# Head of a one-layer trunk kernel: the tiles of x loaded ahead of w_ada, and the sums over w_ada shared out anew between TensorE and VectorE

## The chip, the cores and the metric

One core of one Trainium2 chip runs the kernel. The metric is the device time in microseconds (us). TensorE (PE) multiplies matrices, PEld is its weight load, VectorE is DVE, ScalarE is ACT, GpSimd is POOL, and SP issues the loads from the chip's main memory (DRAM) into SBUF. PSUM is where TensorE writes; it has eight banks.

## The reference

`x` is 1024 x 1024 in float32, `c` one vector of 1024, `w_ada` 1024 x 6144. What follows is the start of the layer; the mixer, the output projection and the MLP come after it and are not touched by the change.

```python
c_act = jax.nn.silu(c)
mod = (c_act @ w_ada[l] + b_ada[l])[:, None, :]
sh_m, sc_m, g_m, sh_f, sc_f, g_f = jnp.split(mod, 6, axis=-1)
u = layer_norm(x) * (1 + sc_m) + sh_m
z = u @ w_in[l]
```

## The kernel before

The order of the work is written out by hand, one program for each engine; semaphores tie them together, and each engine takes its program strictly in order.

`x` comes in eight tiles of 128 rows (512 KB each, in `mid`). For each tile VectorE takes mean and variance (`stats`: two BN_STATS, one BN_AGGR, one small add), ScalarE takes the root (`take_root`), VectorE makes the reciprocal and the negative mean (`scale_bias`), ScalarE normalises the tile (`norm`, 128x1024), TensorE transposes it in eight 128x128 pieces (`transpose_x`), and ScalarE copies the transposed tile from PSUM to `x_t` (`save_tile`). VectorE normalises tile 7 itself and copies it to `x_t`.

`w_ada` comes in twelve chunks of 512 columns (2 MB each) into three buffers `ada[i % 3]`; chunk `i` has eight row blocks `k`. Chunks 0 and 1 are the shift of `u`, chunks 2 and 3 its scale; chunks 0 and 2 belong to the channel blocks k = 0 to 3 of `u`, chunks 1 and 3 to k = 4 to 7. The product with `c_act` is made in one of two ways:

- on TensorE (`row_chunk`): one matmul for each row block, `c_act` as a weight of one column, 512 columns streamed, summed into one row of PSUM; ScalarE saves that row (`save_ada_row`), and four small matmuls turn it into columns (`row_columns`);
- on VectorE (`start_chunk`, `end_chunk`): one 128x512 multiply (or multiply and add) for each row block into `partial`, and four small matmuls against ones sum over the partitions and give the same columns.

Before, chunks 0 and 2 go the first way and chunks 1 and 3 the second. From the columns VectorE makes `mod` (`mixer_columns`), ScalarE makes `u_tmp = x_t * scale + shift` and its rounded half `act_hi` (`modulate_x`), VectorE the rest `act_lo` (`cut_u_lo`). Each of the eight blocks `k` of `u` then enters the first projections: `rows_part(n, k)` is six matmuls of 512 columns (three products for each half of the rows) for weight block `n`, whose own halves come from ScalarE (`cut_hi`) and VectorE (`cut_lo`). So the projections of k = 0 to 3 wait for chunks 0 and 2, those of k = 4 to 7 for chunks 1 and 3.

Of the kernel before, what the change touches and what calls it, by code (L numbers as in the profile page):

```python
# [65 lines left out]
N_DIRECT = 2  # L66
ROW_ORDER = (0, 2, 1, 3)
ADA_BANKS = {0: 0, 2: 1}
# [7 lines left out]
def trunk_layer(nc, x, c, w_ada, b_ada, w_in, b_gate, w_pool, pool_scale, rel_bias, conv_w, conv_b,  # L76
# [173 lines left out]
    with ExitStack() as ctx:  # L250
# [229 lines left out]
        def _(sp):  # L480
# [11 lines left out]
            def load_ada(i):  # L492
                if i == 3:
                    sp.wait_ge(head_ps_done, 1)
                elif i == 4:
                    sp.wait_ge(partial_done, 1)
                elif i == 5:
                    sp.wait_ge(head_ps_done, 4)
                elif i == 6:
                    sp.wait_ge(partial_done, 2)  # L500
                elif i >= 7:
                    sp.wait_ge(partial_done, i - 2 - N_DIRECT)
                if i < 4:
                    load_ada_half(i, 0)
                    load_ada_half(i, 1)
                else:
                    sp.dma_start(ada[i % 3][:, :, :], ada_view[:, :, i * HALF:(i + 1) * HALF])\
                        .then_inc(ada_in[i % 3], 16)

            def load_ada_half(i, half):  # L510
                ks = slice(4 * half, 4 * half + 4)
# [421 lines left out]
        def _(act):  # L933
# [28 lines left out]
            def save_ada_row(i):  # L962
                act.wait_ge(head_ps_done, {0: 1, 2: 4}[i])
                copy(ada_row[i], ps[0:1, ADA_BANKS[i], :]).then_inc(head_sb_done, 1)

            def save_tile(i):
                act.wait_ge(z_done, i + 1)
                copy(x_t[:, :, i * P:(i + 1) * P], tile_banks(i)).then_inc(x_copied, 1)

            for i in range(0, ST, 2):  # L970
                take_root(i, i)
                take_root(i + 1, i + 1)
                norm(i, i, mid[:, i, :])
                if i + 1 < ST - 1:
                    norm(i + 1, i + 1, mid[:, i + 1, :])
                if i == 2:
                    save_ada_row(0)
                if i == ST - 2:
                    save_ada_row(2)
                    cut_hi(0)  # L980
                    save_tile(i)
                else:
                    save_tile(i)
                    save_tile(i + 1)
# [16 lines left out]
            cut_hi(2)  # L1001
            act.wait_ge(mod_done, 2)
# [372 lines left out]
        def _(dve):  # L1375
# [33 lines left out]
            for i in range(0, ST, 2):  # L1409
                for t in (i, i + 1):  # L1410
                    dve.wait_ge(x_in[t], 16)
                    stats(mid[:, t, :], t)
                for t in (i, i + 1):
                    scale_bias(t, t)
                if i == 4:
                    dve.wait_ge(head_ps_done, 3)
                    nc.vector.tensor_copy(cols[:, 0:ROWS_A], ps[:, 7, PIECE:PIECE + ROWS_A])
                    nc.vector.tensor_copy(cols[:, ROWS_A:ROWS_A + ROWS_C], ps[:, 7, PIECE + P:PIECE + P + ROWS_C])\
                        .then_inc(cols_done, 1)
# [8 lines left out]
            def start_chunk(i):  # L1428

                dve.wait_ge(ada_in[i % 3], 16 * (i // 3 + 1))  # L1430
# [4 lines left out]
                link(nc.vector.tensor_scalar(partial_of(i)[:, :], ada[i % 3][:, 0, :], c_act[:, 0:1], None, ALU.mult))  # L1435
                add_rows(i, range(1, 4))

            def end_chunk(i):
                if i in (1, 3):
                    dve.wait_ge(ada_end_in[i % 3], 16 * (i // 3 + 1))  # L1440
                add_rows(i, range(4, 8))
# [42 lines left out]

            mixer_columns(0)
            dve.wait_ge(z_done, ST)
            nc.vector.tensor_copy(x_t[:, :, (ST - 1) * P:ST * P], tile_banks(ST - 1)).then_inc(x_copied, 1)
# [573 lines left out]
        def _(pe):  # L2061
# [19 lines left out]
            def row_chunk(i, half):  # L2081

                pe.wait_ge((ada_in, ada_end_in)[half][i % 3], 16)
                for k in range(4 * half, 4 * half + 4):
                    ins = nc.tensor.matmul(ps[0:1, ADA_BANKS[i], :], c_act[:, k:k + 1], ada[i % 3][:, k, :],  # L2085
                                           start=k == 0, stop=k == 7)
                return ins

            def row_columns(i):

                if i in (0, 2):
                    pe.wait_ge(head_sb_done, 3 + i // 2)
                else:
                    pe.wait_ge(cols_done, 1)
                    pe.wait_ge(partial_done, 1 + i // 2)
                for m in range(4):
                    out, ms = ps[:, 6 + i % 2, 4 * i + m:4 * i + m + 1], slice(m * P, (m + 1) * P)
                    if i in (0, 2):
                        ins = nc.tensor.matmul(out, ada_row[i][:, ms], ones_row[0:1, 0:1], start=True, stop=True)
                    else:  # L2100
                        ins = nc.tensor.matmul(out, partial_of(i)[:, ms], ones_row[:, 0:1], start=True, stop=True)
                ins.then_inc(reduced, 1)
# [28 lines left out]

            pe.wait_ge(head_sb_done, 2)
            row_chunk(0, 0)
            transpose_x(0)
            transpose_x(1)
            row_chunk(0, 1).then_inc(head_ps_done, 1)
            transpose_x(2)
            transpose_x(3)
# [5 lines left out]
            row_chunk(2, 0)  # L2144
            transpose_x(4)
            row_columns(0)
            transpose_x(5)
            row_chunk(2, 1).then_inc(head_ps_done, 1)
            transpose_x(6)
            row_columns(2)  # L2150
            transpose_x(7)
# [416 lines left out]
```

## Time and profile before

| | us |
|---|---|
| median of 3 runs (lowest to highest) | 1427.40 (1426.52 to 1428.69) |
| the profiled execution, its own time | 1426.88 |
| its span | 1425.1 |
| TensorE busy in the span | 1393.0 |
| first matmul of the head, first projection, second restart of the projections (from the span's start) | 7.16, 39.14, 64.58 |

"Busy" counts an instruction from its start to its end; matmuls overlap, so the distance from one matmul's start to the next one's is the better price of one in a row. A float32 matmul appears as two instructions in the trace (four `row_chunk` matmuls are a row with x8); a transpose appears as one.
### The profile page before, as it was taken

The numbers are of one execution on the slowest core, as the hardware profiler recorded it, in microseconds if no ns is written. First come the engines' busy times: TensorE is split into PE (matmuls) and PEld (weight loads), VectorE is DVE, ScalarE is ACT, GpSimd is POOL, SyncE is SP. The second block draws the span as 40 slices with busy tenths as digits, with TensorE's granted clock in tenths as the row PEclk, the third lists the DMA queues.
The fourth block names the chain that finished last, engine by engine and source line by source line (L and its number), as shares of the span: only waits on it lengthen the run. The fifth ranks groups of instructions, "written<-read, shape, count | busy, mean of one in ns | idle before, by whom it ended". The sixth has DMA issues, their size and how long they took to land.

```text
span 1425.1 us, 17299 instructions
## 1 busy us (share of the span) xinstructions
PE 1393.0 (98%) x6522; PEld 1148.6 (81%) x6522; DVE 969.4 (68%) x1340; ACT 647.3 (45%) x914; POOL 421.8 (30%) x453
## 2 busy tenths in 40 slices
PE   7799999999999999999999999999999999999996
PEld 3688888888888888888888888888888888888885
DVE  5789677776479946464768797556565646437787
ACT  5522677777542124101616774443345535343251
POOL 1006465555566000000024327333444200001315
PEclk9899999999999999999999999999999999999998
DMA  9775465654565232762622555444445878456361
GB/s 347 266 266 159 148 185 156 188 168 149 161 234 172 89 104 79 245 192 86 200 114 89 183 181 193 142 145 146 156 163 207 297 277 299 162 211 236 118 222 60
DMA packets 159083, 256.42 MB, mean 180 GB/s; under 512 B 11352, under 2 KB 81422, under 8 KB 159000
## 3 DMA queue, kind: packets, MB, share of 16 engines
q1 hardware_dynamic: 144152, 204.97, 43.1%
q0 software_dynamic: 14848, 50.34, 10.5%
q8 instruction: 52, 0.85, 0.3%
q14 instruction: 31, 0.25, 0.1%
HBM read 182.36 MB, written 68.71 MB: 176 GB/s over the span
## 4 chain that ended last, share of the span: by engine, by line
PE 91%; DVE 5%; ACT 2%; issue 1%; DMA 1%; SPq 0%; DVEq 0%; ACTq 0%
PE ps L2065 24%; PE ps L2067 24%; PE ps L2066 24%; PE ps L2214 11%; PE ps L2254 2%; PE ps L2264 2%; PE ps L2279 2%; PE ps L2085 1%; DVE part_lo L1922 1%; PE ps L2129 1%; PE ps L2404 1%; DVE q L1983 0%; DMA k_raw<-tw_scratch 0%; DMA ada<-in_w_ada_dram 0%; DVE w_lo L1387 0%
## 5 line engine op out<-in xcount | busy, mean ns | idle before, releaser
L2065 PE MATMUL ps<-act_hi,w_hi 128*128 128x512 f32 (+1 forms) x480 | 187.2, 390 | 9.4 <-DVE act_lo L1482 9.4
L1922 DVE TENSOR_TENSOR part_lo<-k_raw,part_hi 128x1024 fp32r<-128x1024 f32 x112 | 146.1, 1332 | 58.6 <-ACT part_hi L935 55.4
L2067 PE MATMUL ps<-act_hi,w_lo 128*128 128x512 f32 (+1 forms) x480 | 184.6, 385 | 0.0
L2066 PE MATMUL ps<-act_lo,w_hi 128*128 128x512 f32 (+1 forms) x480 | 184.6, 385 | 0.0
L2065 PE MATMUL ps<-part_hi 128*128 128x512 f32 x448 | 174.3, 389 | 0.0
L2066 PE MATMUL ps<-part_lo,part_hi 128*128 128x512 f32 x448 | 174.3, 389 | 0.0
L2067 PE MATMUL ps<-part_hi,part_lo 128*128 128x512 f32 x448 | 174.3, 389 | 0.0
L935 ACT ACTIVATE part_hi<-k_raw 128x1024 fp32r<-128x1024 f32 x112 | 116.4, 1059 | 113.6 <-DMA k_raw<-tw_scratch 48.8
L2065 PEld LDWEIGHTS ps<-act_hi,w_hi 128*128 128x128 f32 x480 | 91.1, 190 | 28.4 <-issue 5.9
L1387 DVE TENSOR_TENSOR w_lo<-w_raw,w_hi 128x1024 fp32r<-128x1024 f32 x51 | 65.9, 1291 | 65.6 <-ACT w_hi L935 65.6
L2066 PEld LDWEIGHTS ps<-act_lo,w_hi 128*128 128x128 f32 x480 | 91.2, 190 | 18.4 <-issue 1.0
L2067 PEld LDWEIGHTS ps<-act_hi,w_lo 128*128 128x128 f32 x480 | 90.9, 189 | 17.9
L2214 PE MATMUL ps<-act_hi,w_lo 128*128 128x512 f32 x240 | 99.8, 416 | 0.0
L1311 ACT ACTIVATE h_buf<-h_buf,cols 128x1024 f32<-128x1024 f32 x28 | 32.3, 1152 | 145.6 <-DVE h_buf L1917 145.6
L2214 PE MATMUL ps<-act_hi,w_hi 128*128 128x512 f32 x240 | 95.2, 397 | 3.2 <-DVE kd L1572 3.1
L2067 PEld LDWEIGHTS ps<-part_hi,part_lo 128*128 128x128 f32 x448 | 84.1, 188 | 17.6
L2065 PEld LDWEIGHTS ps<-part_hi 128*128 128x128 f32 x448 | 84.1, 188 | 17.4
L2066 PEld LDWEIGHTS ps<-part_lo,part_hi 128*128 128x128 f32 x448 | 84.1, 188 | 17.4
L2214 PE MATMUL ps<-act_lo,w_hi 128*128 128x512 f32 x240 | 94.4, 393 | 0.0
L935 ACT ACTIVATE w_hi<-w_raw 128x1024 fp32r<-128x1024 f32 x52 | 54.7, 1052 | 84.4 <-PE ps L2067 84.3
L894 POOL TENSOR_TENSOR resid<-resid,q 128x512 f32<-128x512 f32 x16 | 25.3, 1615 | 217.8 <-DVE q L1983 217.8
L2065 PE MATMUL ps<-act_hi,set_hi 128*128 128x512 f32 x224 | 87.1, 389 | 0.0
(260 smaller groups left out, 3202.4 us busy)
## 6 DMA issues: line engine op xcount, KB each, us to landing
k_raw<-h_scratch SPq DMA_DIRECT2D x112, 256.0 KB, 4.2
w_raw<-in_w_in_dram SPq DMA_DIRECT2D x42, 512.0 KB, 4.1
ada<-in_w_ada_dram SPq DMA_DIRECT2D x8, 2048.0 KB, 9.6
tw_rows<-in_w_ff_dram POOLq DMA_DIRECT2D x64, 256.0 KB, 4.1
tw_scratch<-tw_sum POOLq DMA_DIRECT2D x32, 512.0 KB, 3.7
h_scratch<-h_sum POOLq DMA_DIRECT2D x64, 256.0 KB, 3.0
k_raw<-tw_scratch SPq DMA_DIRECT2D x64, 256.0 KB, 5.4
pair_raw<-in_w_ff_dram SPq DMA_DIRECT2D x13, 1024.0 KB, 6.3
```

Source lines behind the costliest of these rows:

```text
L894: nc.gpsimd.tensor_tensor(row, row, quad[:, t % 4, :], ALU.add).then_inc(quad_added, 1)
L935: return nc.scalar.activation(out, in_, ACT.Copy, **kw)
L1311: nc.scalar.activation(row, row, ACT.Relu, bias=cols[:, R_FF1 + n:R_FF1 + n + 1]).then_inc(relu_done, 1)
L1387: nc.vector.tensor_tensor(lo[:, :, :], w_raw[n % 2][:, :, :], f(hi[:, :, :]), ALU.subtract)\
L1922: nc.vector.tensor_tensor(part_lo[s][:, :, :], k_raw[rs][:, :, :], f(part_hi[s][:, :, :]), ALU.subtract)\
L2065: nc.tensor.matmul(out, sh, mh, start=first, stop=False)
L2066: nc.tensor.matmul(out, sh, ml, start=False, stop=False)
L2067: return nc.tensor.matmul(out, sl, mh, start=False, stop=last)
L2214: ins = nc.tensor.matmul(ps[:, hz % 2, :], s, v, start=kk == 0, stop=kk == 23)
L2254: ins = nc.tensor.matmul(ps[:, 4 + part, 0:n], qs[s][:, h, t * P:(t + 1) * P], kd[s][:, term, h, ks], start=term == 0, stop=term == 1)
L2264: ins = nc.tensor.transpose(banks(6)[:, cs], probs[b % 2][:, cs], ident[:, :])
L2279: ins = nc.tensor.matmul(ps[:, 2 + b % 2, 0:2 * P], vs[s][:, t + 1 - nb + m, h * P:(h + 1) * P], pt[:, b % 2, m, :, :], start=m == 0, stop ...
```

## The change

The loads are issued in another order (SP): `c`, then all eight tiles of `x`, then both halves of chunk 0, the small rows, chunk 2 in a piece of six row blocks and one of two, weight blocks 0 and 1, chunk 1, weight block 2, chunk 3. ScalarE and VectorE handle the tiles one at a time with an offset, no longer in pairs; VectorE copies tiles 6 and 7 to `x_t`, and the copy of the small rows to `cols` moves behind that. TensorE takes five transposes first and only then the rows of chunk 0; of chunk 2 it takes six row blocks and VectorE the last two; of chunk 3 it takes four, in the middle of the projections, and VectorE the other four. `row_columns` adds both shares in PSUM. Two of the `rows_part` of weight block 2 move behind the columns of chunks 1 and 3.

```diff
-N_DIRECT = 2
+N_DIRECT = 1
+SPLIT = {0: 4, 1: 4, 2: 6, 3: 4}
...
-ADA_BANKS = {0: 0, 2: 1}
+ADA_BANKS = {0: 0, 2: 1, 3: 6}
...
-            load_ada_half(0, 0)
-            load_x(range(2))
-            load_ada_half(0, 1)
-            load_x(range(2, 4))
+            load_x(range(ST))
+            load_ada(0)
...
-            load_ada_half(2, 0)
-            load_x(range(4, 6))
-            load_ada_half(2, 1)
-            load_x(range(6, ST))
+            load_ada(2)
             load_block(0)
+            load_block(1)
             load_ada(1)
-            load_block(1)
+            load_block(2)
             load_ada(3)
-            load_block(2)
...
-            for i in range(0, ST, 2):
+            for i in range(ST):
                 take_root(i, i)
...
+                if i >= 1:
+                    norm(i - 1, i - 1, mid[:, i - 1, :])
+                if i >= 2:
+                    save_tile(i - 2)
+            save_ada_row(0)
+            save_ada_row(2)
+            cut_hi(0)
...
             cut_hi(2)
+            save_ada_row(3)
             act.wait_ge(mod_done, 2)
...
+            for t in (ST - 2, ST - 1):
+                dve.wait_ge(z_done, t + 1)
+                dve.wait_ge(x_copied, ST - 2)
+                nc.vector.tensor_copy(x_t[:, :, t * P:(t + 1) * P], tile_banks(t)).then_inc(x_copied, 1)
...
+            ada_chunk(2)
             mixer_columns(0)
...
                 for m in range(4):
...
+                    if i != 1:
+                        ins = nc.tensor.matmul(out, ada_row[i][:, ms], ones_row[0:1, 0:1], start=True, stop=i == 0)
+                    if i > 0:
+                        ins = nc.tensor.matmul(out, partial_of(i)[:, ms], ones_row[:, 0:1], start=i == 1, stop=True)
...
+            pe.wait_ge(mod_done, 1)
+            row_chunk(3, 0).then_inc(head_ps_done, 1)
             pe.wait_ge(w_lo_done, 3)
-            for k in range(4):
+            for k in range(2):
                 rows_part(2, k)
             row_columns(1)
             row_columns(3)
+            for k in range(2, 4):
+                rows_part(2, k)
```

TensorE from its first instruction, before (`ident,mid` is a transpose, eight to a tile; `ada` with `c_act` is a row block of `w_ada`; `h_pad` holds the saved rows):

```order
L2085 MATMUL ps<-ada_61,c_act 1x512 x4
L2129 MATMUL ps<-ident,mid 128x128 x16
L2085 MATMUL ps<-ada_61,c_act 1x512 x4
L2129 MATMUL ps<-ident,mid 128x128 x16
L2140 MATMUL ps<-ident,rows_a 128x112
L2142 MATMUL ps<-ident,rows_c 128x62
L2085 MATMUL ps<-ada_63,c_act 1x512 x4
L2129 MATMUL ps<-ident,mid 128x128 x8
L2099 MATMUL ps<-ones_row,h_pad 128x1 x4
L2129 MATMUL ps<-ident,mid 128x128 x8
L2085 MATMUL ps<-ada_63,c_act 1x512 x4
```

TensorE from its first instruction, in the change:

```order
L2132 MATMUL ps<-ident,mid 128x128 x40
L2087 MATMUL ps<-ada_61,c_act 1x512 x4
L2132 MATMUL ps<-ident,mid 128x128 x16
L2087 MATMUL ps<-ada_61,c_act 1x512 x4
L2132 MATMUL ps<-ident,mid 128x128 x8
L2144 MATMUL ps<-ident,rows_a 128x112
L2146 MATMUL ps<-ident,rows_c 128x62
L2087 MATMUL ps<-ada_63,c_act 1x512 x6
L2102 MATMUL ps<-ones_row,h_pad 128x1 x5
L2104 MATMUL ps<-ones_row,partial_66 128x1
```

Five tiles of transposes now stand ahead of the first row block, and all of chunk 2's rows and all of the first columns stand behind the last transpose.

ScalarE from its fourth instruction on, in the change (`mid` is the normalisation, `x_t` the copy of a transposed tile, `rstd` the root):

```order
L949 ACTIVATE rstd<-rstd 128x1 x2
L954 ACTIVATE mid<-mid,neg_mean,rstd 128x1024
L949 ACTIVATE rstd<-rstd 128x1
L954 ACTIVATE mid<-mid,neg_mean,rstd 128x1024
L933 ACTIVATE x_t<-ps 128x8x128
L949 ACTIVATE rstd<-rstd 128x1
L954 ACTIVATE mid<-mid,neg_mean,rstd 128x1024
L933 ACTIVATE x_t<-ps 128x8x128
```

A root, a normalisation and a copy now alternate for every tile, where pairs of each stood before; the normalisation of tile 4 has the copies of three earlier tiles ahead of it.

## Rows read from the trace of the kernel before

**Rows 1.** The page: busy time by engine, and the chain's shares by engine

```profile
PE 1393.0 (98%) x6522; PEld 1148.6 (81%) x6522; DVE 969.4 (68%) x1340; ACT 647.3 (45%) x914; POOL 421.8 (30%) x453
...
PE 91%; DVE 5%; ACT 2%; issue 1%; DMA 1%; SPq 0%; DVEq 0%; ACTq 0%
```

**Rows 2.** TensorE's waits, whole span: us in total, times, longest us

```profile
PE ps L2065 <- DVE act_lo L1482: 9.4, 3, 4.7
PE ps L2085 <- DMA ada<-in_w_ada_dram: 7.2, 1, 7.2
```

**Rows 3.** Chain of waits, first 130 us: start us, us, what

```profile
1.21 5.82 DMA ada<-in_w_ada_dram
7.16 6.40 PE ps L2085 x8
...
19.12 1.90 PE ps L2129 x16
21.31 3.52 PE ps L2085 x8
24.84 1.02 PE ps L2129 x8
...
32.41 0.98 PE ps L2099 x8
```

**Rows 4.** Timeline at TensorE's first pause: start us, us, instruction [idle before <-releaser]

```profile
33.49 0.17 DVE L1472 TENSOR_TENSOR mod<-ps,cols 128x8 f32<-128x8 f32 x1 [2.98 <-PE ps L2099]
...
34.44 1.23 DVE L1487 COPY x_t<-ps 128x1024 f32<-128x1024 f32 x1 [0.58 <-PE ps L2129]
...
35.77 2.37 ACT L989 ACTIVATE u_tmp<-x_t,mod 128x1024 f32<-128x1024 f32 x2 [1.91 <-DVE x_t L1487]
...
39.14 0.77 PE L2065 MATMUL ps<-act_hi,w_hi 128*128 128x512 f32 x1 [4.74 <-DVE act_lo L1482]
```

**Rows 5.** Timeline from there to TensorE's second pause

```profile
48.86 0.50 PE L2065 MATMUL ps<-act_hi,w_hi 128*128 128x512 f32 x1 [0.56 <-DVE act_lo L1482]
...
53.40 5.47 DVE L1446 SCALAR_TENSOR_TENSOR partial<-ada,c_act,partial 128x512 f32<-128x512 f32 x7
...
58.59 1.84 PE L2101 MATMUL ps<-ones_row,partial 128*128 128x1 f32 x16
...
60.95 1.24 ACT L989 ACTIVATE u_tmp<-x_t,mod 128x1024 f32<-128x1024 f32 x1 [15.37 <-DVE mod L1474]
...
64.58 0.80 PE L2065 MATMUL ps<-act_hi,w_hi 128*128 128x512 f32 x1 [4.15 <-DVE act_lo L1482]
...
67.31 0.47 PE L2065 MATMUL ps<-act_hi,w_hi 128*128 128x512 f32 x1
```

**Rows 6.** Timeline of the tiles of x: their statistics, normalisation, copy, root

```profile
8.43 1.29 DVE L1393 BATCH_NORM_STATS2 bn<-mid 128x6 f32<-128x512 f32 x2 [5.64 <-DMA mid<-in_x_dram]
...
12.08 2.37 ACT L956 ACTIVATE mid<-mid,neg_mean,rstd 128x1024 f32<-128x1024 f32 x2
...
13.71 1.29 DVE L1393 BATCH_NORM_STATS2 bn<-mid 128x6 f32<-128x512 f32 x2 [1.30 <-DMA mid<-in_x_dram]
...
15.34 1.27 DVE L1393 BATCH_NORM_STATS2 bn<-mid 128x6 f32<-128x512 f32 x2
...
20.18 1.94 ACT L935 ACTIVATE x_t<-ps 128x1024 f32<-128x1024 f32 x2
...
22.00 0.20 ACT L951 ACTIVATE rstd<-rstd 128x1 f32<-128x1 f32 x1
```

**Rows 7.** Stretches: length, PE, PEld, DVE, ACT, POOL busy (x), PEclk, DMA share, GB/s

```profile
36.80:39.10 2.30, 0.00 (x0) 0.00 (x0) 1.92 (x2) 2.27 (x3) 0.00 (x0) 0.50 1.05 381
39.10:43.40 4.30, 4.26 (x10) 3.42 (x11) 2.20 (x2) 4.27 (x5) 0.00 (x0) 0.50 1.07 351
...
64.60:67.30 2.70, 2.70 (x6) 2.13 (x7) 2.58 (x4) 2.67 (x3) 0.00 (x0) 0.50 1.05 387
...
190.70:192.39 1.69, 0.00 (x0) 0.03 (x1) 1.41 (x4) 1.17 (x4) 0.00 (x0) 1.00 1.01 367
```

More of the change, by code:

```diff
@@ L495, in load_ada @@
                 elif i == 4:
-                    sp.wait_ge(partial_done, 1)
+                    sp.wait_ge(partial_done, 2)
                 elif i == 5:
                     sp.wait_ge(head_ps_done, 4)
+                    sp.wait_ge(partial_done, 1)
                 elif i == 6:
-                    sp.wait_ge(partial_done, 2)
+                    sp.wait_ge(head_ps_done, 5)
+                    sp.wait_ge(partial_done, 3)
                 elif i >= 7:
@@ L510, in load_ada_half @@
             def load_ada_half(i, half):
-                ks = slice(4 * half, 4 * half + 4)
+                ks = (slice(0, SPLIT[i]), slice(SPLIT[i], 8))[half]
                 sp.dma_start(ada[i % 3][:, ks, :], ada_view[:, ks, i * HALF:(i + 1) * HALF])\
@@ L962, in save_ada_row @@
             def save_ada_row(i):
-                act.wait_ge(head_ps_done, {0: 1, 2: 4}[i])
+                act.wait_ge(head_ps_done, {0: 1, 2: 4, 3: 5}[i])
                 copy(ada_row[i], ps[0:1, ADA_BANKS[i], :]).then_inc(head_sb_done, 1)
@@ L1408, in _ @@
             dve.wait_ge(head_sb_done, 2)
[L1409 to L1419, printed above, removed]
+            for t in range(ST):
+                dve.wait_ge(x_in[t], 16)
+                stats(mid[:, t, :], t)
+                if t >= 1:
+                    scale_bias(t - 1, t - 1)
+            scale_bias(ST - 1, ST - 1)
             dve.wait_ge(norm_ready, ST)
@@ L1428, in start_chunk @@
             def start_chunk(i):
-                dve.wait_ge(ada_in[i % 3], 16 * (i // 3 + 1))
+                if i == 1:
+                    dve.wait_ge(ada_in[1], 16)
+                elif i in (2, 3):
+                    dve.wait_ge(ada_end_in[i % 3], 16 * (i // 3 + 1))
+                else:
+                    dve.wait_ge(ada_in[i % 3], 16 * (i // 3 + 1))
                 if i == 4:
@@ L1434, in start_chunk @@
                     dve.wait_ge(reduced, i - 3)
-                link(nc.vector.tensor_scalar(partial_of(i)[:, :], ada[i % 3][:, 0, :], c_act[:, 0:1], None, ALU.mult))
-                add_rows(i, range(1, 4))
+                k0 = SPLIT[i] if i in (2, 3) else 0
+                link(nc.vector.tensor_scalar(partial_of(i)[:, :], ada[i % 3][:, k0, :], c_act[:, k0:k0 + 1], None,
+                                             ALU.mult))
+                add_rows(i, range(k0 + 1, 4))
             def end_chunk(i):
-                if i in (1, 3):
-                    dve.wait_ge(ada_end_in[i % 3], 16 * (i // 3 + 1))
-                add_rows(i, range(4, 8))
+                if i == 1:
+                    dve.wait_ge(ada_end_in[1], 16)
+                add_rows(i, range({2: 7, 3: 5}.get(i, 4), 8))
             def add_rows(i, ks):
@@ L2081, in row_chunk @@
             def row_chunk(i, half):
-                pe.wait_ge((ada_in, ada_end_in)[half][i % 3], 16)
-                for k in range(4 * half, 4 * half + 4):
+                pe.wait_ge((ada_in, ada_end_in)[half][i % 3], 32 if i == 3 else 16)
+                for k in range(4 if half else 0, 8 if half else SPLIT[i]):
                     ins = nc.tensor.matmul(ps[0:1, ADA_BANKS[i], :], c_act[:, k:k + 1], ada[i % 3][:, k, :],
-                                           start=k == 0, stop=k == 7)
+                                           start=k == 0, stop=k == (7, None, 5, 3)[i])
                 return ins
             def row_columns(i):
-                if i in (0, 2):
-                    pe.wait_ge(head_sb_done, 3 + i // 2)
-                else:
+                if i != 1:
+                    pe.wait_ge(head_sb_done, {0: 3, 2: 4, 3: 5}[i])
+                if i > 0:
+                    pe.wait_ge(partial_done, {2: 1, 1: 2, 3: 3}[i])
+                if i in (1, 3):
                     pe.wait_ge(cols_done, 1)
-                    pe.wait_ge(partial_done, 1 + i // 2)
                 for m in range(4):
                     out, ms = ps[:, 6 + i % 2, 4 * i + m:4 * i + m + 1], slice(m * P, (m + 1) * P)
[L2098 to L2101, printed above, removed]
+                    if i != 1:
+                        ins = nc.tensor.matmul(out, ada_row[i][:, ms], ones_row[0:1, 0:1], start=True, stop=i == 0)
+                    if i > 0:
+                        ins = nc.tensor.matmul(out, partial_of(i)[:, ms], ones_row[:, 0:1], start=i == 1, stop=True)
                 ins.then_inc(reduced, 1)
@@ L2130, in transpose_x @@
                 ins.then_inc(z_done, 1)
+            for i in range(5):
+                transpose_x(i)
             pe.wait_ge(head_sb_done, 2)
             row_chunk(0, 0)
-            transpose_x(0)
-            transpose_x(1)
+            transpose_x(5)
+            transpose_x(6)
             row_chunk(0, 1).then_inc(head_ps_done, 1)
-            transpose_x(2)
-            transpose_x(3)
+            transpose_x(7)
             pe.wait_ge(small_in, SMALL_ROWS)
@@ L2143, in _ @@
                 .then_inc(head_ps_done, 1)
[L2144 to L2145 removed]
+            row_chunk(2, 0).then_inc(head_ps_done, 1)
             row_columns(0)
[L2147 to L2149 removed]
             row_columns(2)
[L2151 removed]
             def rows_part(n, k):
```

19 lines of the change are left out of this document (4 added, 15 removed).

## The prediction

> **What bounds the kernel now.** I read the page first: TensorE is busy for 1393.0 of 1425.1 us, and 91% of the chain that ended last runs through it [rows 1]. The rest must be looked for in its pauses, so the second view is who TensorE waited for. Two entries carry the head: 7.2 us until the first piece of `w_ada` has landed, and three waits of 9.4 us in all for `act_lo`, the last piece of a block of `u` [rows 2]. The chain of waits then shows how TensorE spends the time between: from 7.16 us it works without a gap through rows of `w_ada` (`L2085`), transposes (`L2129`) and columns (`L2099`), the first four row matmuls in 6.40 us, later fours in 3.52 us [rows 3]. Third, the timeline at the pauses: the last transpose is done at 34.4, VectorE's copy of tile 7 holds ScalarE's first `u_tmp` until 35.77, and the first projection starts at 39.14 [rows 4]; the columns of chunks 1 and 3 start at 58.59, `u_tmp` for the next block at 60.95, and the projections start again at 64.58 [rows 5]. From 64.58 on TensorE hardly waits until the end of the kernel, so whatever moves the end of this stretch moves the whole time one for one. I therefore work out two distances: from the start to the first projection (39.14 now), and from there to the second restart (25.44 now, plus what a slow clock costs behind it).
>
> **First distance, the tiles.** In the old order the first 1 MB of `w_ada` lands at 1.21 + 5.82 = 7.03 us [rows 3]; tile 2, which has 2.5 MB queued behind that point up to its own end, starts its statistics at 13.71 after a wait for the load [rows 6]. That is 2.62 million bytes in 6.68 us, 1.34 us for a tile of 512 KB, and 7.03 + 1.34 = 8.4 agrees with tile 0's 8.43 [rows 6]. With x first, tile 0 should land one such step before the old 1 MB did, at 5.7 us (an estimate), and tile 7 at 15.1. From tile 0's arrival to its normalisation the trace has 8.43 to 12.08, 3.65 us, with the statistics of two tiles in it [rows 6]; the new program has the same two ahead of it, so tile 0 is normalised from 9.35, and tile 1 from about 11.4, one more tile of statistics (13.71 to 15.34, 1.63 us, and about 0.4 for reciprocal and mean) later.
>
> From there ScalarE sets the pace, not the load: for each tile 1.19 for the normalisation (2.37 for two), 0.97 for the copy (1.94 for two) and up to 0.20 for the root [rows 6], 2.3 us against 1.34 for a load and 2.0 for VectorE. Tile 4 is normalised at 11.4 + 3 x 2.3 = 18.3 to 19.5, and its transpose ends TensorE's first group at 20.5. In the old program TensorE had been at work since 7.16; now it starts at 10.6 and stands idle for more than half of the time between two tiles. All rows of `w_ada` are behind this group in its program. Chunk 0's first half lands at 5.7 + 4.72/0.392 = 17.7 (seven tiles and 1 MB later), so the rows wait for the tiles, by 2.8 us. The rest of the loads is on time: six blocks of chunk 2 land near 25, weight block 0 near 28, against uses at 30.4 and 37.
>
> **First distance, TensorE's queue.** What stands between 20.5 and the columns: eight row matmuls of chunk 0, 2 x 3.52; tiles 5, 6, 7, 3 x 1.02; the two small transposes, 21.31 - (19.12 + 1.90) = 0.29; six row matmuls of chunk 2, 6 x 0.88 = 5.28; columns of chunk 0, 0.98; columns of chunk 2, now eight matmuls, 1.96 [rows 3]. The sum is 18.6, and nothing of it is waited for: tile 5 and tile 6 are normalised by 22 and 24, tile 7 by 24, the saved row of chunk 2 costs ScalarE about 0.6 us, which chunk 0's columns cover. So the columns are done at 39.1, where the old program had them at 33.39. VectorE's two blocks of chunk 2 (1.3 us by seven of 0.78 in 5.47 [rows 5]) and the copies of tiles 6 and 7 lie beside the rows and are done before 34; if they were late they would cost at most their 3.8 us. The copy that held up `u_tmp` by 1.9 us after `mod` [rows 4] is thus off the path. From the end of the columns to the end of `mod` is about 0.5 us (33.39 to 33.49, then two steps of some 0.2), and from `u_tmp` to the first projection 39.14 - 35.77 = 3.37 [rows 4]: 39.1 + 0.5 + 3.4 = 43.0. **First term: +3.9 us.** Its bounds: if tile 0 lands 1 us earlier or ScalarE's pace is VectorE's 2.0, the rows start at 19.5, and no earlier than their landing at 17.7, so +1.1 is the lowest; if the transposes run at half speed with the rows behind them, see below.
>
> The 2.0 us that the slow clock cost behind the first restart (39.10 to 43.40 at 0.50 [rows 7]) stays as it is: TensorE pauses for 3.9 us instead of 4.7, and ran into a wait for `act_lo` at 48.86 anyway [rows 5], which hides most of it either way.
>
> **Second distance.** The old one is 39.14 to 58.59 (19.45), columns 1.84, and 4.15 of pause [rows 5]. VectorE's four blocks of chunk 3 fewer (4 x 0.78 = 3.1 us) would help only if VectorE ended last there. Its seven blocks ended at 58.87 (53.40 + 5.47), when TensorE had got to the columns anyway, so that gain is cover, not path. On TensorE: 12 of the projection matmuls move behind the columns, at (58.59 - 48.86)/42 = 0.23 each (42 run without a gap between these two starts), so -2.78 ahead of the columns; four row matmuls of chunk 3 come in, +3.52; chunk 3's columns are eight instead of four, +0.98. The columns end at 19.45 - 2.78 + 3.52 + 1.84 + 0.98 = 23.01, and `u` of the next block is ready 4.15 later, at 27.16, with 1.4 us of idle time left after the 12 matmuls. Against 25.44 that is +1.72. In return the clock should stay up: the old pause of 4.15 was followed by 2.70 us at 0.50 [rows 7], in which six matmuls took 64.58 to 67.31, 2.73 against 1.38, and a pause of 1.69 us at 190.7 left it at 1.00 [rows 7]. **Second term: +1.72 - 1.35 = +0.4 us**; between -0.2 (nothing idle in the pause and the fill better than counted) and +1.8 (clock falls all the same).
>
> **Sum.** +4.3 us on the profiled execution's own 1426.88 gives 1431.2; its span would go from 1425.1 to about 1429.4. That execution lies 0.5 below the median of the runs, so for the median the forecast is 1427.4 + 4.3 = 1431.7.
>
> **Rivals.** *A slow clock among the transposes.* TensorE works for 1.02 of every 2.3 us between tiles; the clock may fall to 1.2 GHz there and TensorE enter the rows so. For it: the pause after 34.4, with nothing running, had the clock at 0.50 by 36.8, and four row matmuls at the slow level took 6.40 instead of 3.52 [rows 3, 7]. Against it: 1.69 us of idle time at 190.7 changed nothing [rows 7], and the pauses here are 1.3 us. Price: up to +2.9 in the rows, so 1433 to 1434.5. The Trainium skill, page TensorE: Matmul & The Clock Gate, section A second HAM failure mode: psum-queue depth-cycling, says that short idle times between groups of matmuls, often enough, make the clock swing between its levels; by that rule this rival would be the forecast, and the pause at 190.7 alone does not bear it out.
>
> *Not slower: the rows start when they land.* If ScalarE gets through a tile faster than counted (its copies overlap the roots, tile 0 lands early), the fifth transpose ends near 17.7 and TensorE's rows start there, 2.8 us earlier: +1.1 in the first term, +0.4 in the second, 1428.9, which a measurement cannot tell from no change (about 0.2%, 2.9 us, is what it can tell). It decides at one point: whether the first row matmul is held by the landing of chunk 0 or by the transpose before it. Against it: 2.37 and 1.94 for two are distances in a row with nothing between, so they already hold what overlap there is.
>
> *The change does not do what it says.* The split of chunk 3 takes work from VectorE ahead of the second pause; if VectorE's chain to `act_lo` still ends late, or the 12 matmuls run out and the clock falls, the second term is +1.8 and the time 1433. And a gain would need TensorE's queue to cost nothing: then the landing of chunk 2's six blocks, near 25, would lead, with 5.3 of rows and 2.9 of columns behind it the columns would be there at 33.2, the first projection at 37.1, the first term -2.0 and the time 1425.8, which is still no difference that can be told. A gain beyond that has no mechanism that I see.
>
> **How the numbers follow.** Forecast (+2.9 to +5.5): 0.56. Slow clock in the rows or at the second restart: 0.19. Rows start on landing: 0.18. A queue that costs nothing, or a gain that I don't see: 0.07. Range: from the landing rival's 1428.9, a little lowered to 1428.3, to the slow clock in the rows together with a part of the second, 1435.5. Slower by over 0.2% is the first two nearly whole, 0.73; within 0.2% 0.22; faster 0.05.
>
> **What would show it.** In the profile of the changed kernel: the first statistics at 5.7; the first transposes near 10.6 and at steps of 2.3; the first row matmul near 20.5 right behind a transpose; the first projection near 43.0; a second pause of about 1.4 us with PEclk at 1.00 behind it, 27 us after the first projection. It is wrong if the row matmuls run before 18 us, if the columns are there before 36, or if the second distance is under 25.

## The result, and the profile after

The changed kernel takes 1433.49 us (median of 7 runs, 1431.27 to 1437.33) beside 1427.40 of the kernel before (7 runs, 1426.52 to 1428.69): a ratio of 1.0044, 95% interval 1.0033 to 1.0054. It is 6.1 us slower. Forecast were 1431.7 us, 1428.3 to 1435.5, and slower with 0.73.

The profiled execution took 1433.49 us, its span is 1431.7. The page, as [rows 1]: busy time by engine and the chain's shares.

```profile
PE 1398.0 (98%) x6542; PEld 1153.8 (81%) x6542; DVE 972.1 (68%) x1339; ACT 646.6 (45%) x914; POOL 422.8 (30%) x453
...
PE 90%; DVE 5%; ACT 2%; issue 1%; DMA 1%; SPq 0%; DVEq 0%; ACTq 0%
```

TensorE's waits, as [rows 2]. The 7.2 us for the first piece of `w_ada` are gone, a wait of 10.0 us for the first normalised tile stands in their place:

```profile
PE ps L2132 <- ACT mid L954: 12.6, 4, 10.0
PE ps L2067 <- DVE act_lo L1477: 5.7, 3, 4.1
```

The chain of waits has the first tile's load (start us, us, what), which lands at 4.91:

```profile
1.21 3.70 DMA mid<-in_x_dram
```

The head in the timeline of the changed kernel (start us, us, instruction, idle time before and its releaser), as [rows 3, 4, 6]. The tiles pace TensorE until 18.57; from 19.59 it runs without a gap through rows, transposes and columns, and the first projection starts at 43.09 instead of 39.14:

```profile
5.01 1.29 DVE L1386 BATCH_NORM_STATS2 bn<-mid 128x6 f32<-128x512 f32 x2 [2.21 <-DMA mid<-in_x_dram]
...
10.03 3.77 PE L2132 MATMUL ps<-ident,mid 128*128 128x128 f32 x16 [10.03 <-ACT mid L954]
14.31 1.10 PE L2132 MATMUL ps<-ident,mid 128*128 128x128 f32 x8 [0.50 <-ACT mid L954]
16.44 1.09 PE L2132 MATMUL ps<-ident,mid 128*128 128x128 f32 x8 [1.03 <-ACT mid L954]
18.57 1.09 PE L2132 MATMUL ps<-ident,mid 128*128 128x128 f32 x8 [1.04 <-ACT mid L954]
19.59 3.59 PE L2087 MATMUL ps<-ada,c_act 128*1 128x512 f32 x8
...
29.85 5.31 PE L2087 MATMUL ps<-ada,c_act 128*1 128x512 f32 x12
35.09 1.05 PE L2102 MATMUL ps<-ones_row,h_pad 1*128 1x1 f32 x8
...
38.36 0.59 PE L2104 MATMUL ps<-ones_row,partial 128*128 128x1 f32 x2
39.05 0.17 DVE L1467 TENSOR_TENSOR mod<-ps,cols 128x8 f32<-128x8 f32 x1 [6.67 <-PE ps L2104]
...
39.72 2.37 ACT L981 ACTIVATE u_tmp<-x_t,mod 128x1024 f32<-128x1024 f32 x2 [2.98 <-DVE mod L1469]
...
43.09 0.77 PE L2067 MATMUL ps<-act_hi,w_hi 128*128 128x512 f32 x1 [4.15 <-DVE act_lo L1477]
```

The second pause, as [rows 5]. Columns start at 63.50; those of chunk 3 alternate between one row (L2102) and 128 rows (L2104) of input and follow each other at 0.31 us. The first projection matmul of block 2 that was moved starts at 66.79, the pause after the twelve is 1.27 us, the restart is at 71.09:

```profile
63.50 0.94 PE L2104 MATMUL ps<-ones_row,partial 128*128 128x1 f32 x8
64.38 0.38 PE L2102 MATMUL ps<-ones_row,h_pad 1*128 1x1 f32 x2
64.69 0.38 PE L2104 MATMUL ps<-ones_row,partial 128*128 128x1 f32 x2
...
66.79 0.49 PE L2067 MATMUL ps<-act_hi,third_hi 128*128 128x512 f32 x1
...
67.44 1.25 ACT L981 ACTIVATE u_tmp<-x_t,mod 128x1024 f32<-128x1024 f32 x1 [6.10 <-DVE mod L1469]
...
71.09 0.50 PE L2067 MATMUL ps<-act_hi,w_hi 128*128 128x512 f32 x1 [1.27 <-DVE act_lo L1477]
```

Stretches, as [rows 7] (length, then busy time of PE, PEld, DVE, ACT, POOL, then PEclk, DMA share, GB/s). The record of the clock starts at 13.9 us; ahead of it sixteen transposes took 3.77 us, behind it eight took 1.10, so the first two tiles ran at the low level. From there the clock stayed up over the pauses among the transposes, fell at 37.8 among the columns (0.85 in their mean), was low into the first products (up to 48.1), and was up behind the second restart, where the kernel before had 0.50. A new low stretch stands at 198, in the attention stage:

```profile
13.60:19.50 5.90, 3.32 (x25) 2.57 (x24) 5.56 (x19) 5.90 (x10) 0.00 (x0) 1.00 1.06 376
...
35.10:39.00 3.90, 3.85 (x25) 3.66 (x24) 0.00 (x0) 1.53 (x2) 0.00 (x0) 0.85 0.00 0
...
43.10:47.60 4.50, 4.50 (x11) 3.57 (x12) 2.44 (x3) 4.44 (x6) 0.00 (x0) 0.50 1.07 381
...
71.10:75.00 3.90, 3.90 (x17) 3.25 (x18) 3.76 (x6) 3.10 (x3) 0.00 (x0) 1.00 1.05 387
198.00:201.00 3.00, 2.81 (x7) 2.30 (x8) 1.97 (x5) 1.36 (x3) 2.19 (x4) 0.54 0.69 169
```

So the second restart is 6.5 us later (71.09 against 64.58), and the span is 6.6 us longer: 1360.6 us follow the restart, 1360.5 before.

### The profile page after: what moved, and what is told of

The parts are those of the page before. It is cut to its first block, busy times and chain, and to the rows that moved or that the text cites. A ratio compares the mean times of both kernels' runs of the same rounds, so it can differ in the third digit from the quotient of the medians.

```text
span 1431.7 us, 17344 instructions
## 1 busy us (share of the span) xinstructions
PE 1398.0 (98%) x6542; PEld 1153.8 (81%) x6542; DVE 972.1 (68%) x1339; ACT 646.6 (45%) x914; POOL 422.8 (30%) x453
## 4 chain that ended last, share of the span: by engine, by line
PE 90%; DVE 5%; ACT 2%; issue 1%; DMA 1%; SPq 0%; DVEq 0%; ACTq 0%
PE ps L2067 24%; PE ps L2069 23%; PE ps L2068 23%; PE ps L2217 11%; PE ps L2257 2%; PE ps L2267 2%; PE ps L2282 2%; PE ps L2087 1%; DVE part_lo L1924 1%; PE ps L2407 0%; DVE q L1985 0%; DMA k_raw<-tw_scratch 0%; PE ps L2132 0%; DVE w_lo L1380 0%; DVE bn L1386 0%
```

## The experiments

All were run in five rounds beside the kernel before (medians 1427.93 for the first four, 1427.55 for the next four, 1427.26 for the last). The three columns of times in the table are read in each trace as above: the start of the first projection, the distance from there to the second restart, and what follows to the end of the span. They come from one profiled execution of each kernel, the median from all of its executions, and the two can differ: the profiled one took 1431.35 us in e7 and 1432.34 in e8, against medians of 1433.93 and 1435.03.

| kernel | first projection | to second restart | rest | median us | ratio to before, 95% interval |
|---|---|---|---|---|---|
| before | 39.14 | 25.44 | 1360.5 | 1427.4 | |
| changed | 43.09 | 28.00 | 1360.6 | 1433.49 | 1.0044, 1.0033 to 1.0054 |
| e0, changed, again | 42.65 | 28.13 | 1361.1 | 1433.56 | 1.0042, 1.0029 to 1.0054 |
| e1, before + moved matmuls | 38.92 | 25.21 | 1358.3 | 1425.92 | 0.9988, 0.9979 to 0.9997 |
| e2, changed, chunk 3 on VectorE | 43.89 | 25.12 | 1358.8 | 1429.31 | 1.0011, 1.0002 to 1.0020 |
| e4, changed, old loads | 47.61 | 29.26 | 1360.8 | 1438.35 | 1.0076, 1.0063 to 1.0088 |
| e5, e1 + three orders | 38.13 | 23.03 | 1360.6 | 1422.17 | 0.9963, 0.9951 to 0.9975 |
| e6, changed, chunk 2 on TensorE | 42.72 | 29.59 | 1359.1 | 1433.34 | 1.0038, 1.0026 to 1.0050 |
| e7, changed, pause filled | 43.04 | 28.21 | 1358.4 | 1433.93 | 1.0042, 1.0029 to 1.0055 |
| e8, changed, rows earlier | 43.25 | 28.14 | 1359.2 | 1435.03 | 1.0050, 1.0036 to 1.0063 |
| e9, e1 + split of chunk 3 | 39.10 | 27.99 | 1360.8 | 1429.84 | 1.0017, 1.0008 to 1.0026 |

**The changed kernel again.**

> The changed kernel once more, for another execution's trace and more times. Theory: first projection at 43.1 and the second restart 28.0 later, the same in each execution within 0.5 us; the spread of the times (1431.3 to 1437.3) goes with the granted clock, so the stretch of slow clock at 198 us is gone or stands elsewhere, and the time is about 1431.5 where it is gone. Rival: the stretch at 198 us is there again, a fixed cost of the change.

Measured: 1433.56 us. The two distances come back within 0.5 us. The low stretch at 198 is not there; instead the clock fell at 66.4, where the last column of chunk 3 ended and the first moved matmul began, and most of the moved matmuls ran at half speed inside the pause, as the stretch shows:

```profile
66.10:69.50 3.40, 3.40 (x11) 2.75 (x11) 0.48 (x3) 2.48 (x3) 0.00 (x0) 0.54 1.05 386
71.00:75.00 4.00, 4.00 (x19) 3.31 (x18) 3.88 (x5) 3.11 (x4) 0.00 (x0) 1.00 1.05 388
```

The restart is at full clock all the same, and the time is no shorter without the stretch at 198: the 1431.5 us expected then did not come, since this execution waited longer elsewhere (1361.1 us behind the restart; see the part on the clock below). The 6 us are in the two distances, 6.2 us of them here (70.78 against 64.58 for the restart), 6.5 in the first trace.

**The moved matmuls alone**, on the kernel before:

```diff
-            for k in range(4):
+            for k in range(2):
                 rows_part(2, k)
             row_columns(1)
             row_columns(3)
+            for k in range(2, 4):
+                rows_part(2, k)
```

> The kernel before with one part of the change: of weight block 2, the products for k = 2 and 3 (12 matmuls) stand behind the columns of chunks 1 and 3. Theory (the two distances): first projection at 39.1 as before; the columns of chunk 3 now wait for VectorE's partial, which ends near 58.9, so the second restart comes near 63.9 (24.8 after the first), with 1.4 us of idle time left and PEclk at 1.00 behind it: -0.7 for the restart and -1.3 for the clock, 1425.4. Rival (the second pause costs nothing that comes back, or the clock falls anyway): 1427.4.

Measured: 1425.92 us, 2.0 below the kernel before in the same runs (1427.93). VectorE becomes late: TensorE reaches the columns of chunk 3 earlier and waits for its share, which the kernel before had in hand.

```profile
58.82 1.02 PE L2101 MATMUL ps<-ones_row,partial 128*128 128x1 f32 x8 [2.19 <-DVE partial L1446]
```

The two distances give only 0.45 of the 2.0 us. Behind the restart the clock is at 1.00, and the thirteenth matmul from it starts 2.74 us later (66.87) where the kernel before has 4.18 (68.76): 1.44 us, where 1.3 were expected for the clock. So the move is the one part that gains, and 2.2 us of VectorE's chain lie bare behind it. That is the time that a split of chunk 3 could have won at most.

**Chunk 3 wholly on VectorE again**, in the changed kernel:

```diff
-            pe.wait_ge(mod_done, 1)
-            row_chunk(3, 0).then_inc(head_ps_done, 1)
...
-            save_ada_row(3)
...
-                k0 = SPLIT[i] if i in (2, 3) else 0
+                k0 = SPLIT[i] if i == 2 else 0
...
-                add_rows(i, range({2: 7, 3: 5}.get(i, 4), 8))
+                add_rows(i, range(7 if i == 2 else 4, 8))
```

> The change without its share of chunk 3 on TensorE: all eight row blocks of chunk 3 on VectorE, as before; the rest as in the change. Theory (TensorE ends last in the second distance, so four row matmuls and four more column matmuls there cost their own time): first projection at 43.1, second restart 24.9 later instead of 28.0, and the time near 1430.4. Rival (VectorE's chain ends last there, and the share on TensorE is cover): no change against the changed kernel, 1433.5, or later.

Measured: 1429.31 us, second distance 25.12 instead of 28.00. The wait for VectorE is back (2.11 us), and it is cheaper than TensorE's share was:

```profile
63.68 1.05 PE L2102 MATMUL ps<-ones_row,partial 128*128 128x1 f32 x8 [2.11 <-DVE partial L1439]
```

**The split of chunk 3 alone**, on e1, that is with the loads, tiles and chunks 0 and 2 of the kernel before:

```diff
+            pe.wait_ge(mod_done, 1)
+            row_chunk(3, 0).then_inc(head_ps_done, 1)
             pe.wait_ge(w_lo_done, 3)
...
+            save_ada_row(3)
...
+                k0 = 4 if i == 3 else 0
...
-                add_rows(i, range(4, 8))
+                add_rows(i, range(5 if i == 3 else 4, 8))
```

> The kernel before with the second distance of the change alone: chunk 3 split between TensorE (four row matmuls, and columns of two heights) and VectorE (four blocks), and the twelve moved matmuls. Loads, tiles, chunk 0 and chunk 2 are those of the kernel before. Theory (the two distances add up, and the split of chunk 3 lengthens the second one wherever the first ends): first projection at 38.9 to 39.2 us, second restart 27.7 to 28.2 us after it (25.44 before, 25.21 with the fill alone), 1428.3 to 1429.7 us: 2.5 to 3.8 us over the 1425.9 of the fill alone. Rival (the second distance of the changed kernel is long only because of what the new first part leaves behind on VectorE and ScalarE): second distance 25.2 to 26.5, 1426 to 1427.2 us.

Measured: 1429.84 us; second distance 27.99, the changed kernel's own, though it begins 4 us earlier:

```profile
39.10 0.76 PE L2072 MATMUL ps<-act_hi,w_hi 128*128 128x512 f32 x1 [4.74 <-DVE act_lo L1489]
...
59.51 0.94 PE L2108 MATMUL ps<-ones_row,partial 128*128 128x1 f32 x8
...
67.09 0.50 PE L2072 MATMUL ps<-act_hi,w_hi 128*128 128x512 f32 x1 [1.27 <-DVE act_lo L1489]
```

With e0, e1 and e2 this is a table of two by two. Against the kernel before in the same runs, e1 is 2.0 us below, e2 1.4 above, e9 2.6 above and e0 5.6 above. Over e1 the new first part thus costs 3.4 us (e2), the split of chunk 3 costs 4.6 (e9), both 7.6 (e0): they add up to within 0.4. In the head alone the split is 2.8 us (27.99 against 25.21); the traces have more of it in the rest, 1360.8 in e9, with a stretch at half clock from 194.1 on, and 1358.3 in e1, without one.

**The old loads in the changed kernel**, with TensorE's first rows ahead of the tiles again:

```diff
-            load_x(range(ST))
-            load_ada(0)
+            load_ada_half(0, 0)
+            load_x(range(2))
+            load_ada_half(0, 1)
+            load_x(range(2, 4))
...
             row_chunk(2, 0).then_inc(head_ps_done, 1)
+            for i in range(4, ST):
+                transpose_x(i)
             row_columns(0)
```

> The change with the old order of loads (first half of chunk 0 ahead of x, and so on) and TensorE's rows of chunk 0 first again, as before; the shares of chunks 2 and 3, the handling of the tiles one at a time and the moved products stay as in the change. Theory (the first distance is TensorE's queue, which starts late when the rows stand behind the tiles): first projection near 37.5 instead of 43.1, the second restart 28.0 later, the time near 1428. Rival (not the order but the new shares cost the time): first projection near 43, 1433.

Measured: 1438.35 us, a miss by 10 us; first projection at 47.61. A new chain, in its timeline: chunk 2's rows stand ahead of tile 4's transpose, so ScalarE's copy of tile 4 waits 3.49 us; the root of tile 7 stands behind that copy, VectorE waits 4.37 us for it, and the last block of chunk 2, which VectorE takes up only after its copies of tiles 6 and 7, holds the columns:

```profile
25.90 5.31 PE L2092 MATMUL ps<-ada,c_act 128*1 128x512 f32 x12
...
32.27 1.02 ACT L938 ACTIVATE x_t<-ps 128x1024 f32<-128x1024 f32 x1 [3.49 <-PE ps L2137]
33.20 0.19 ACT L954 ACTIVATE rstd<-rstd 128x1 f32<-128x1 f32 x1
...
33.42 0.16 DVE L1399 RECIPROCAL rstd<-rstd 128x1 f32<-128x1 f32 x1 [4.37 <-ACT rstd L954]
...
39.69 0.35 PE L2107 MATMUL ps<-ones_row,h_pad 1*128 1x1 f32 x2 [2.07 <-DVE partial L1446]
```

The run does not isolate the load order, since tile by tile handling does not fit the old order of rows. What the load order costs by itself stays open.

**Chunk 2 wholly on TensorE**, in the changed kernel:

```diff
-            row_chunk(2, 0).then_inc(head_ps_done, 1)
+            row_chunk(2, 0)
+            row_chunk(2, 1).then_inc(head_ps_done, 1)
...
-            ada_chunk(2)
             mixer_columns(0)
```

> The changed kernel with chunk 2 wholly on TensorE: blocks 6 and 7 become two more row matmuls, VectorE has no share of chunk 2, and its columns take one pass each instead of two of different heights. Load order, tile handling, the split of chunk 3 and the moved matmuls stay. Theory (the columns of two heights cost 3.8 us where 2.9 were summed, and TensorE ends the first distance): two more row matmuls at 0.88 us add 1.77 us ahead, the four passes that go and the wait for one ScalarE copy bring the columns to some 1.5 to 2 us behind the rows' end, so the first projection comes 0.3 to 0.7 us earlier than 43.09, at 42.4 to 42.8, second distance 28.0, 1432.8 to 1433.2 us: the split of chunk 2 gained nothing. Rival (the columns cost no more than a pass of one height, the split spares TensorE its two matmuls): first projection at 44.0 to 44.9, 1434.4 to 1435.3 us.

Measured: first projection at 42.72, inside the theory's 42.4 to 42.8 and far from the rival's 44.0. It is not earlier than in every execution of the changed kernel: e0 has 42.65. Two more row matmuls, and yet the columns are done at 38.83, between the 38.95 of the changed kernel's first trace and the 38.50 of e0, since eight columns of one height take 1.94 us where twelve, eight of them in mixed rows, take 3.44 (e0) to 3.86:

```profile
29.94 7.03 PE L2085 MATMUL ps<-ada,c_act 128*1 128x512 f32 x16
36.89 1.94 PE L2100 MATMUL ps<-ones_row,h_pad 1*128 1x1 f32 x16
42.72 0.76 PE L2065 MATMUL ps<-act_hi,w_hi 128*128 128x512 f32 x1 [3.88 <-DVE act_lo L1476]
```

The split of chunk 2 gained nothing; what TensorE saved in rows it paid in columns. The time (1433.34) is the changed kernel's: in this execution the second distance was 29.59, because the clock fell among the columns at 65.3 and the moved matmuls took longer than the pause.

**Rows one transpose earlier**, in the changed kernel:

```diff
-            for i in range(5):
+            for i in range(4):
                 transpose_x(i)
             pe.wait_ge(head_sb_done, 2)
             row_chunk(0, 0)
+            transpose_x(4)
             transpose_x(5)
```

> The changed kernel with the first four row matmuls one transpose earlier in TensorE's order, behind tile 3's transpose instead of tile 4's. Chunk 0's first blocks had landed by 17.7 us; in the changed kernel the rows began at 19.59. Theory (from the rows' start on TensorE is the queue that sets the first projection): rows start at 17.5 to 17.9 us instead of 19.59, with the pause of 1.04 us ahead of tile 4's transpose gone, columns and first projection 0.8 to 1.1 us earlier (42.0 to 42.3), and the time 0.8 to 1.1 us less, 1432.4 to 1432.7 us. Rival (ScalarE's pace of the tiles sets it, and tile 4's transpose, now at 21.3 instead of 18.57, delays the copies of the tiles behind it): first projection at 43 us or later, 1433.5 us or more.

Measured: 1435.03 us, first projection 43.25: the rival. The rows start 1.98 us earlier; 1.02 go to tile 4's transpose, which now stands behind them, and 1.46 to a wait for ScalarE, whose copy of tile 4 comes later (22.27 instead of 20.54) and with it the normalisation of tile 6, so the columns start at 35.67 instead of 35.09:

```profile
17.61 3.59 PE L2087 MATMUL ps<-ada,c_act 128*1 128x512 f32 x8
21.14 1.97 PE L2132 MATMUL ps<-ident,mid 128*128 128x128 f32 x16
24.56 1.09 PE L2132 MATMUL ps<-ident,mid 128*128 128x128 f32 x8 [1.46 <-ACT mid L954]
...
35.67 1.27 PE L2102 MATMUL ps<-ones_row,h_pad 1*128 1x1 f32 x10
```

So ScalarE's pace of the tiles and TensorE's queue bind together; to start one earlier alone wins nothing.

**The pause ahead of the first projection filled** with transposes that the kernel has no use for:

```diff
             row_columns(2)
+            for _ in range(12):
+                nc.tensor.transpose(ps[:, 1, 0:P], ident[:, :], ident[:, :])
```

> The changed kernel with twelve identity transposes into a bank that nobody reads any more, behind chunk 2's columns, in TensorE's pause ahead of the first projection (38.95 to 43.09 us), where the granted clock was 0.50. They add work that the kernel needs for nothing. Theory (the slow clock there costs nothing, since TensorE waits for VectorE's fourth low part 9.7 us behind the first projection at either clock): first projection unchanged at 43.1 us, the clock back up earlier than 47.69, the wait for the fourth low part longer than 0.32 us by what the faster clock saves, second distance 28.0 and the time the same within 0.1% (1433.5 us). Rival (the slow clock of the first 4.6 us of products is on the path): 1.5 to 2.3 us less, 1431.2 to 1432 us.

Measured: 1433.93 us, first projection 43.04, second distance 28.21: no change, as the theory had it. The filling did not keep the clock up: it fell at 39.2, while TensorE was busy in every moment. It rose again at 46.0, and the low part is waited for 0.76 us, where the changed kernel's first trace has 48.1 and 0.32; but that is not the filling, since e0, without it, has 45.9 and 0.79. Stretches of one us in its trace:

```profile
38.00:39.00 1.00, 1.00 (x8) 0.97 (x9) 0.00 (x1) 0.00 (x0) 0.00 (x0) 1.00 0.00 0
39.00:40.00 1.00, 1.00 (x8) 1.00 (x7) 0.71 (x3) 0.34 (x1) 0.00 (x0) 0.58 0.00 0
```

**The moved matmuls with three orders changed**, on e1, without anything else of the change:

```diff
-            row_columns(2)
             transpose_x(7)
+            row_columns(2)
...
-            mixer_columns(0)
             dve.wait_ge(z_done, ST)
             nc.vector.tensor_copy(x_t[:, :, (ST - 1) * P:ST * P], tile_banks(ST - 1)).then_inc(x_copied, 1)
+            mixer_columns(0)
...
+            start_chunk(1)
             cut_lo(1)
             cut_u_lo(2)
-            start_chunk(1)
```

> The kernel before with the twelve moved matmuls of block 2 (as in the run that adds the fill alone) and three orders changed: tile 7's transpose ahead of chunk 2's columns on TensorE, VectorE's copy of tile 7 ahead of its mixer columns, and chunk 1's share of VectorE started one step earlier, ahead of block 1's low part. Nothing of the split, of the load order or of the tile-by-tile handling is in it. Theory (the waits of both heads end on VectorE and ScalarE, and what is put ahead of them there moves the end): first projection at 38.5 us (38.92 with the fill alone), second restart 23.2 to 23.8 us after it (25.21 with the fill alone), 1423.2 to 1424 us. Rival (the moved steps only change which wait is last, since ScalarE's cuts or the landing of chunk 1 come as late): the same as the fill alone, 1425.9 us.

Measured: 1422.17 us, ratio 0.9963 (0.9951 to 0.9975), 5.4 us below the kernel before beside it, and some 11 below the changed one. The first projection comes 1.0 us earlier, the second restart 2.4 us earlier after it, and the wait for chunk 3's share of VectorE has shrunk from 2.19 to 0.45:

```profile
38.13 0.76 PE L2065 MATMUL ps<-act_hi,w_hi 128*128 128x512 f32 x1 [3.97 <-DVE act_lo L1482]
...
55.98 1.02 PE L2101 MATMUL ps<-ones_row,partial 128*128 128x1 f32 x8 [0.45 <-DVE partial L1446]
...
59.88 1.23 DVE L1482 TENSOR_TENSOR act_lo<-u_tmp,act_hi 128x1024 fp32r<-128x1024 f32 x1 [2.40 <-ACT act_hi L935]
...
61.16 0.66 PE L2065 MATMUL ps<-act_hi,w_hi 128*128 128x512 f32 x1
```

The trace shows no wait ahead of 61.16, but that does not make TensorE the only bound: the clock fell at 58.1, so the last of the moved matmuls ran at half speed and filled the time up to 61.1, and `act_lo` was ready at 61.11 (59.88 + 1.23). Both end together.

## Why the prediction was right

**The structure held.** The time follows the second restart: 1358.3 to 1361.1 us come behind it in all eleven traces, however long the head was. Slower, by the sum of two distances, is what happened. The span grew by 6.6 us where 4.3 were summed: 0.84 more come from the second distance, and about 1.4 are the gain of the clock, which the end of the span does not show. Both are taken up below.

**First distance: +3.95 against +3.9, but by errors that cancel.** Tile 0 landed at 4.9, not at 5.7 (statistics at 5.01), so the rows started at 19.59 and not at 20.5: 0.9 early. As forecast, the rows waited for the transpose and not for their landing, which came at 16.6 (17.7 forecast); so the condition of the rival "rows start when they land" was not met. The queue behind it was summed at 18.6 and took 38.95 - 19.59 = 19.4: the columns were priced at 2.94 and took 3.86. About 0.5 of that is that columns of two heights follow each other at 0.31 us, and about 0.4 that the last of them ran at half the clock: in e0, where the clock stayed up, the columns took 3.44. From the columns' end to the first projection it was 4.14 against 3.9. That the sum came out to 0.05 us is luck: in e0, the same kernel, the term is +3.5.

**Rows as the bound: only half the truth.** The prediction took TensorE's queue from 20.5 on as the path with nothing waited for. e8 shows that ScalarE's pace lies close under it: rows 1.98 us earlier did not bring the first projection forward (43.25 against 43.09 and 42.65).

**Second distance: +2.56 against +1.72.** The columns started 20.41 after the first projection (20.19 summed), took 3.29 (2.82 summed, the same two heights), and 4.30 passed from their end to the restart (4.15 summed): 0.22 + 0.47 + 0.15 = 0.84. The step that failed is the price of a column matmul in a mixed row, taken from the 0.23 and 0.245 of rows of one height [rows 3, 5]; it was 0.31. Whether the change of height makes it dearer, or that two matmuls write the same column of PSUM, no run separates. e9 and e2 confirm what the split costs in this distance: with it 28.0, without it 25.1 to 25.2, wherever the first distance ends. That VectorE's relief "is cover, not path" was right for the kernel before, where it ended as TensorE got there; with the moved matmuls VectorE was 2.2 us late (e1), and the split buys these 2.2 with 3.52 of rows and 1.45 more of columns.

**The clock behind the second restart: right in place, and its gain lost again later.** PEclk was 1.00 from 71.10 on, where [rows 7] have 0.50, and the pause left is 1.27 us (1.4 forecast). The 1.35 us that this should give back are there: TensorE runs the same instructions behind the restart in all eleven traces, and the thirteenth of them starts 4.18 us behind it in the kernel before and 2.85 in the changed one. They are lost in the attention stage. There TensorE waits for two tiles, `probs` and then `kd`, for `probs` longer than before, and behind these waits the clock fell, from 198.3 to 201.7. First the kernel before, then the changed one:

```profile
68.76 0.39 PE L2065 MATMUL ps<-act_hi,third_hi 128*128 128x512 f32 x1
...
190.02 0.44 PE L2264 MATMUL ps<-ident,probs 128*128 128x128 f32 x2 [0.24 <-ACT probs L935]
...
192.39 0.47 PE L2214 MATMUL ps<-act_hi,w_hi 128*128 128x512 f32 x1 [1.69 <-DVE kd L1572]
...
73.94 0.39 PE L2067 MATMUL ps<-act_hi,third_hi 128*128 128x512 f32 x1
...
195.82 0.44 PE L2267 MATMUL ps<-ident,probs 128*128 128x128 f32 x2 [0.88 <-ACT probs L933]
...
198.19 0.70 PE L2217 MATMUL ps<-act_hi,w_hi 128*128 128x512 f32 x1 [1.70 <-DVE kd L1574]
```

Counted from the restart, the changed kernel is still 0.71 us ahead at 198.19 (127.10 against 127.81), and 0.84 behind when the clock is up again. So 1360.6 against 1360.5 is a gain, a larger loss, and 0.7 us less between the last matmul and the end of the span. The other traces agree: 1358.3 to 1359.2 us follow the restart where the clock does not fall again while TensorE works (e1, e2, e6, e7, e8), 1360.6 to 1360.8 where it falls in the attention stage (changed, e4, e5, e9). e0, with 1361.1 and no such fall, waits longer: 0.73 us for `probs`, 1.11 and 1.16 for `kd` at 254.05 and 310.45 where the changed kernel's first trace has 0.71 and 0.70, and 0.88 for `w_lo` at 838.59 where that trace has no wait. Why the waits and the clock in the attention stage differ from execution to execution stays open; the length of the waits does not decide it, since the clock fell behind 0.41 and 1.70 us in e5 and stayed up behind 1.09 and 1.69 in e6.

The forecast reason, that the filled pause keeps the clock up, holds in two traces only (the changed kernel's first and e9). In the other eight with the moved matmuls the clock fell among the last columns or behind them, ahead of the restart, and most of these matmuls ran at half speed. In e0, e1, e2, e7 and e8 the pause covers that, and in e5 `act_lo` ends with it; in e4 and e6, where the clock was low from 70.9 to 77.7 and from 65.3 to 72.2, it cost about 1.3 and 1.6 us (29.26 and 29.59 against 28.0).

**The rivals.** A slow clock among the transposes and in the rows did not happen in the changed kernel's first trace: 1.00 from 13.9 to 19.50 over pauses of 0.50, 1.03 and 1.04 us, and four row matmuls in 3.5 us. The Trainium skill, page TensorE: Matmul & The Clock Gate, section A second HAM failure mode: psum-queue depth-cycling, tells of a kernel in which short, frequent idle times between groups of matmuls swing the clock; the changed kernel's first trace does not agree, that of e2 does: there the same transposes ran at 0.53 from 17.0 to 20.4. Its clock was back when the rows began, 1.2 us later than in the changed kernel, 0.4 of it because the first tile came later. In e0, the same kernel as the changed one, tiles 2 and 3 took 1.97 us each instead of 1.10, half speed, and cost nothing: TensorE's waits between the tiles shrank to 0.16 and 0.20, and the rows started at 19.56. The price of up to 2.9 us, for rows at half speed, was paid in no trace: behind the transposes four row matmuls took 3.5 us in all of them. That the 2.0 us of slow clock behind the first restart are hidden by the wait for `act_lo` was right: the wait at 52.82 is 9.73 us behind the first projection, 9.72 before [rows 4, 5], and 9.72 in e0, though the clock was up again 2.2 us earlier there (45.9 against 48.1).

## What to carry to other kernels

Price a matmul by a row of its own neighbourhood: a column matmul in a row of one height is not the same matmul between two heights. Before work is shared out between two engines, move what fills the pause and look at which engine is late then; here three changes of order gave 3.4 us on top of the moved matmuls (e5 against e1, each against the kernel before beside it), where work shared out to the busiest engine cost 4.6 (e9 against e1). When a sum comes out right to 0.1, compare its terms: here a start 0.9 too early and a queue 1.0 too long had cancelled. When a gain is missing at the end of the span, follow the same instruction through both traces from the point where the gain should arise; it can be there and be lost later.

## What the runs showed of the hardware

The granted clock can fall while TensorE is at work without a gap. It fell among one-column matmuls in the changed kernel (37.8 us, 3.85 of 3.90 us busy around it) and in e6 (65.3), at their end in e0 (66.4), and among identity transposes in e7 (39.2); in e9 it stayed at 1.00 through the same columns of chunk 3. One-column float32 matmuls follow each other at 0.22 to 0.25 us where all have one height of input, at 0.31 where one row and 128 rows alternate, two into each column, both at 1.00. Executions of one kernel differ in their mean granted clock, and mostly in time with it: three of e1's took 1423.8 to 1425.1 us at 0.994, one 1428.95 at 0.991; but in e7 four at 0.994 differ by up to 2.9 us. A tile of 512 KB, issued first, landed 3.70 us after its issue in the changed kernel (3.62 to 4.13 in all traces that begin so), 1 MB issued first 5.82 us in the kernel before [rows 3] (5.43 to 6.35).
